# A two-layer decoder trunk in float32: the compression products packed into both column halves of the array

## The reference, cut to what matters

```
kv = (hn @ kv_w).reshape(B, S, 6, 4, 64)            # k_c = kv[:, :, 0], v_c = kv[:, :, 1]
n_cmp = (256 - 32) // 16 + 1                        # 15 blocks of 32 positions, 16 apart
idx = np.arange(n_cmp)[:, None] * 16 + np.arange(32)[None, :]
blocks = a[:, idx] + pos[None, None, :, None, :]    # a is k_c or v_c
blocks = blocks.transpose(0, 3, 1, 2, 4).reshape(B, 4, n_cmp, 32 * 64)
return jax.nn.silu(blocks @ w1) @ w2                # w1: 2048 x 256, w2: 256 x 64
```

## Time and profile before

| | |
|---|---|
| median of three executions | 1446.66 us |
| the profiled execution | 1446.41 us |
| its span (first to last record) | 1444.6 us |
| mean granted TensorE clock | 0.994 |
| PE, PEld, DVE, ACT, POOL busy | 96%, 54%, 30%, 20%, 5% of the span |
| chain that ended last | PE 73%, DMA 11%, SP's queue 10%, DVE 4% |

### The profile page before, as it was taken

How to read it: one execution, slowest core, us unless ns; L and a number is a source line. 1 busy time by engine, 2 the same in 40 slices (tenths; PEclk the granted TensorE clock), 3 DMA queues, 4 the chain that set the end, 5 groups by cost and what they waited for, 6 DMA issues and landing times.

```text
span 1444.6 us, 30800 instructions
## 1 busy us (share of the span) xinstructions
PE 1383.6 (96%) x13835; PEld 780.8 (54%) x13835; DVE 436.7 (30%) x668; ACT 292.7 (20%) x544; POOL 73.8 (5%) x124
## 2 busy tenths in 40 slices
PE   7999899999999898999979999999999999999986
PEld 6888778888777655334233254354354354336423
DVE  1489755554676834110100110110110210101020
ACT  4644444443643521000000000000000000000000
POOL 2000100000012001001001001001001001000100
PEclk9999999999999998999999999999999999999999
DMA  9423495547521806999999999999999999998997
GB/s 359 161 97 117 133 295 175 182 159 185 154 85 44 357 1 243 405 417 388 406 420 400 421 418 401 420 419 399 421 419 391 420 419 406 421 368 305 378 420 287
DMA packets 113123, 444.83 MB, mean 308 GB/s; under 512 B 11117, under 2 KB 37782, under 8 KB 82266
## 3 DMA queue, kind: packets, MB, share of 16 engines
q1 hardware_dynamic: 106160, 431.92, 76.8%
q0 software_dynamic: 3872, 10.49, 2.0%
q10 hardware_dynamic: 2954, 0.40, 0.2%
HBM read 433.85 MB, written 8.92 MB: 306 GB/s over the span
## 4 chain that ended last, share of the span: by engine, by line
PE 73%; DMA 11%; SPq 10%; DVE 4%; issue 1%; POOL 0%; ACT 0%; DVEq 0%; POOLq 0%; ACTq 0%
PE bank L2408 30%; PE bank L2415 10%; DMA ring<-in_moe_w_gu 9%; PE bank L2016 8%; SPq L622 5%; PE bank L2033 4%; SPq L618 4%; PE bank L1886 4%; PE bank L1927 3%; PE bank L2102 2%; DMA ring<-in_moe_w_down 2%; PE bank L2278 2%; PE bank L1908 2%; PE bank L1960 1%; PE bank L2172 1%
## 5 line engine op out<-in xcount | busy, mean ns | idle before, releaser
L2408 PE MATMUL bank<-ring,xT 128*32 128x384 f32 (+1 forms) x5888 | 559.5, 540 | 10.6 <-DMA ring<-in_moe_w_gu 10.4
L2408 PEld LDWEIGHTS bank<-ring,xT 128*32 128x32 f32 x5888 | 186.1, 110 | 378.6 <-issue 325.6
L2415 PE MATMUL bank<-ring,arena 128*32 128x256 f32 x5152 | 284.9, 380 | 16.9 <-DMA ring<-in_moe_w_down 16.9
L1788 DVE TENSOR_TENSOR arena<-arena,bank 128x384 f32<-128x384 f32 (+1 forms) x46 | 27.3, 593 | 734.6 <-PE bank L2408 734.6
L2415 PEld LDWEIGHTS bank<-ring,arena 128*32 128x32 f32 x5152 | 162.9, 110 | 141.2 <-DMA ring<-in_moe_w_down 31.5
L1303 DVE TENSOR_TENSOR ring_lo<-ring,f_whi 128x1024 fp32r<-128x1024 f32 x66 | 80.6, 1225 | 74.4 <-ACT f_whi L915 74.4
L1128 ACT ACTIVATE arena<-bank 128x384 f32<-128x384 f32 (+1 forms) x46 | 25.0, 544 | 380.6 <-PE bank L2408 380.6
L1134 ACT ACTIVATE arena<-bank 128x256 f32<-128x256 f32 x22 | 8.5, 385 | 452.6 <-PE bank L2415 452.0
L915 ACT ACTIVATE f_whi<-ring 128x1024 fp32r<-128x1024 f32 x66 | 69.8, 1062 | 78.4 <-PE bank L2016 48.1
L1886 PE MATMUL bank<-xT,ring 128*128 128x256 f32 x256 | 55.7, 380 | 0.0
L725 POOL DMA_DIRECT2D y_rows<-arena x28 | 15.1, 545 | 750.8 <-ACT arena L1134 750.8
(11 more groups left out here) (312 smaller groups left out, 1183.1 us busy)
## 6 DMA issues: line engine op xcount, KB each, us to landing
ring<-in_moe_w_gu SPq DMA_DIRECT2D x128, 1024.0 KB, 23.9
ring<-in_moe_w_down SPq DMA_DIRECT2D x112, 1024.0 KB, 27.1
ring<-in_moe_w_gu SPq DMA_DIRECT2D x128, 768.0 KB, 24.3
ring<-in_ffn_w_gu SPq DMA_DIRECT2D x22, 1024.0 KB, 7.8
ring<-in_hgrn_w_in SPq DMA_DIRECT2D x16, 1024.0 KB, 15.3
ring<-in_ffn_w_down SPq DMA_DIRECT2D x10, 1024.0 KB, 6.1
ring<-in_kv_w SPq DMA_DIRECT2D x6, 1024.0 KB, 6.3
ring<-in_hgrn_w_out SPq DMA_DIRECT2D x4, 1024.0 KB, 6.2
```

The source lines that it names most:

```text
L2408: last = mm(bank[32 * j:32 * j + 32, b, 0:WIDE[c]], m_xt[:, x, g, k, :], w[:, WIDE[c] * j:WIDE[c] * j + WIDE[c]], start=k == 0, stop=k == ...
L2415: last = mm(bank[32 * j:32 * j + 32, y, 0:256], m_t[c][:, g, b, :], w[:, b % 2, 256 * j:256 * j + 256], start=c == 0 and b == 0, stop=c == ...
```

## The change

There are five edits.

1. The products of odd j are written to partitions 64 to 123 of the same PSUM banks, that is, they use columns 64 to 123 of the array; even j stay in columns 0 to 59. Each half adds up 16 positions.
2. ACT copies both halves (60 x 256 each, for keys and values four copies where there were two silus) into `b_hs`, without the silu.
3. The four transposes (L2154) become four float32 products with all 128 partitions of `b_hs`: the moving operand is a constant of 60 columns, `C_FOLD`, with a one in row p and column p mod 64. It turns the tile and adds the halves. The constant makes the table `cf`, loaded at the start, 60 columns wider (from 631 to 691 floats in a row).
4. Partitions 60 to 63 and 124 to 127 of `b_hs` would enter that product, so DVE clears `b_hs` (128 x 512 floats) behind the additions of L1483, and ACT waits for it (`init_ok` 3).
5. The silu is done by ACT behind the product that turns (two of them, 128 x 120), straight into `b_hid`. DVE's two copies (L1501) are gone, and PE waits for `hid_ready` 2 from ACT.

```
@@ constants
-C_ALL = C_ONE + 1
+C_FOLD = C_ONE + 1
+C_ALL = C_FOLD + NG * NCMP
+    f[:, C_FOLD:C_FOLD + NG * NCMP] = p[:, None] % DH == np.arange(NG * NCMP)[None, :]
@@ ACT
             for kv in range(2):
                 act.wait_ge(hid_ps, kv + 1)
-                act.activation(b_hs[0:NG * NCMP, kv, :], bank[0:NG * NCMP, 4 + kv, 0:CH], ACT.Silu).then_inc(hs_ready, 1)
+                act.wait_ge(init_ok, 3)
+                for o in (0, DH):
+                    last = act.activation(b_hs[o:o + NG * NCMP, kv, :], bank[o:o + NG * NCMP, 4 + kv, 0:CH], ACT.Copy)
+                last.then_inc(hs_ready, 1)
+            act.wait_ge(hsT_ps, 2)
+            for kv in range(2):
+                act.activation(b_hid[:, kv, :, :].rearrange("p n (g c) -> p n g c", g=NG)[:, :, :, 0:NCMP],
+                               bank[:, 3, 256 * kv:256 * kv + 256].rearrange("p (n x) -> p n x", n=2)[:, :, 0:NG * NCMP]
+                               .rearrange("p n (g c) -> p n g c", g=NG), ACT.Silu).then_inc(hid_ready, 1)
@@ DVE
             last.then_inc(cin_ready, 1)
+            dve.wait_ge(cin_ready, 1)
+            dve.memset(b_hs, 0.0).then_inc(init_ok, 1)
             weight_low(12, 13)
...
             dve.wait_ge(init_ok, 2)
-            dve.wait_ge(hsT_ps, 2)
-            for kv in range(2):
-                last = dve.tensor_copy(
...
-            last.then_inc(hid_ready, 1)
@@ PE
-                    last = mm(bank[0:NG * NCMP, 4 + kv, 0:CH], b_cin[ps, j, :, :].rearrange("p g c -> p (g c)"),
-                              w[ps, j % 16, :], start=j == 0, stop=j == CB - 1)
+                    o = DH * (j % 2)
+                    last = mm(bank[o:o + NG * NCMP, 4 + kv, 0:CH], b_cin[ps, j, :, :].rearrange("p g c -> p (g c)"),
+                              w[ps, j % 16, :], start=j < 2, stop=j >= CB - 2)
...
-                    last = tp(bank[:, 3, P * n:P * n + NG * NCMP], b_hs[0:NG * NCMP, kv, P * half:P * half + P],
-                              ident[0:NG * NCMP, 0:NG * NCMP])
+                    last = mm(bank[:, 3, P * n:P * n + NG * NCMP], b_hs[:, kv, P * half:P * half + P],
+                              cf[:, C_FOLD:C_FOLD + NG * NCMP], start=True, stop=True)
...
-            pe.wait_ge(hid_ready, 1)
+            pe.wait_ge(hid_ready, 2)
```

More of the change, by code:

```diff
@@ L1498, in _ @@
             dve.wait_ge(init_ok, 2)
-            dve.wait_ge(hsT_ps, 2)
-            for kv in range(2):
-                last = dve.tensor_copy(
-                    b_hid[:, kv, :, :].rearrange("p n (g c) -> p n g c", g=NG)[:, :, :, 0:NCMP],
-                    bank[:, 3, 256 * kv:256 * kv + 256].rearrange("p (n x) -> p n x", n=2)[:, :, 0:NG * NCMP]
-                    .rearrange("p n (g c) -> p n g c", g=NG))
-            last.then_inc(hid_ready, 1)
             query_sums(0)
```

## The result

The changed kernel takes 1450.83 us in the median of 15 executions (1447.29 to 1452.53), the kernel before in the same sessions 1446.81 (1445.19 to 1449.75). The ratio of the times is 1.0019, 95% interval 1.001 to 1.0027: it is slower, by about 2.7 us by the ratio (the two medians lie 4.0 us apart; I go by the ratio, which comes with an interval). The forecast was 1444.2, faster. The profiled execution took 1451.04 us, its span is 1449.2.

The account below looks back on a forecast made before the run. Experts are bound by their weight stream, their start by PE's chain before it: query(0) 2.64 us earlier, plus 0.1 at the start, gives -2.5 us, so 1443.9 profiled and 1444.2 median; range over the cases 1442.8 to 1447.5.

Parts of the forecast that it names:

- What bounds the kernel: Experts' stage: bound by streaming weights; its start hangs on PE's chain, so each microsecond query(0) starts earlier is passed on.
- The compression products: Compression products on PE: 128 records in four array quarters take 7.0 us instead of 13.96, ending at 416.9.
- Rival A: Compression products: the four tiles don't run together, products stay at 14.0 us; 1447.3 us, chance 0.10.
- rival D: Compression products: four tiles together are slower than two, 18 us; 1451.5 us, chance 0.03.
- The wait for key 3: PE before key_turn(3): stands 3.8 us for DVE's last copy of key 3, which the clearing delays by 0.55 us.
- The product that turns: Between gates and query(0): eight float32 records replacing four transposes take 0.90 us instead of 0.39.
- The copies, the silu and the table load: On ACT: hidden, with cover of 2.4 us for the copies and over 4 us for the silu.
- The start: Load of the constant table, 9.5% wider: costs 0 to 0.6 us, taken as 0.1.
- From there: PE from key_turn(3) to query(0): gates keep 3.60 us, turning product 0.90; query(0) starts at 426.15, 2.64 us earlier.
- rival B: PE's wait near 421 us halves the clock: 1445.7 if short, 1451.2 if long; chance 0.16.
- the long fall: Clock low for 14 us after PE's wait: 4.5 us slower than before, 1451.2 us; chance 0.04.
- the short case: Clock low for about 3 us after PE's wait: gain shrinks to 1.0 us, 1445.7 us; chance 0.12.

Follow-up runs that it names:

- e1_fill: Changed kernel with seven unused float32 products filling PE's standstill before key_turn(3); 1445.07 us, ratio 0.9985 to the kernel before.
- e9_order: Kernel before, unpacked and without clearing, in the PE, DVE and ACT order of e8_mixed; 1447.12 us, ratio 0.9996 to the kernel before.
- e3_unpacked: Changed kernel with all positions' products in columns 0 to 59 again, the rest of the change kept; 1447.61 us, ratio 1.0006 to the kernel before.
- e4_gates: Changed kernel with the gate products moved ahead of key_turn(3), into the standstill; 1445.74 us, ratio 0.9987 to the kernel before.
- e5_chain: e4_gates with DVE's clearing moved behind key 3's last copy and key 2's copy moved earlier; 1442.39 us, ratio 0.9965 to the kernel before.
- e2_half: Kernel before with the compression products of odd positions left out, 64 records instead of 128; 1448.43 us, ratio 1.001 to the kernel before.
- e8_mixed: Changed kernel reordered, halves of query(0) alternating with gates and key_turn(3) on PE, DVE and ACT reordered too; 1441.85 us, ratio 0.9957 to the kernel before.

## Why the prediction was wrong

*What bounds the kernel*: right. The experts are bound by their weights, and what delays or hastens PE at the end of `query(0)` arrives at their start within 0.7 us in the profiles of all six versions that have `query(0)` in one piece (in the changed kernel 3.8 us at the one, 3.4 at the other). The differences of the profiles and of the ratios in the table also go together within 0.7 us, but for e1_fill and e9_order.

*The compression products*: right. 7.07 us for 128 records, 0.055 a record, against the 7.0 forecast from the strips. Rival A and rival D are gone. By the Trainium skill, "TensorE: Matmul & The Clock Gate", in its part on packing tiles, loads overlap running products only when the row group differs. Two of the four tiles here share each row group, the 128 loads lie within 6.68 us beside the products, and the rate still doubled, so the measurement decides against that rule for this shape.

*The wait for key 3*: right, in place, cause and size: 3.60 us, forecast 3.8, ended by the copy forecast; the clearing costs 0.61, forecast 0.55.

*The product that turns*: right, 0.88 (e3_unpacked), forecast 0.90. *The copies, the silu and the table load*: hidden as said; ACT's four copies, 1.55 us, first matter in e4_gates and e5_chain, where PE waits 0.5 us for them. *The start*: the table's piece of the chain is 6.08 us after and 6.36 before, so a cost of 0.1 is not to be seen.

*From there*: wrong, and this is the step that failed. It counted on a granted clock of 1.00 behind the wait, and let the gates keep 3.60 us, the product that turns 0.90 and `query(0)` its 5.66. They took 6.71, 1.69 and 7.85, together 6.1 us more, for the clock was at half during all of the first two and 5.0 us of the third: 3.1 in the gates, 0.8 in the product that turns, 2.2 in `query(0)`. The forecast of -2.6 us and these 6.1 make +3.5; measured at the end of `query(0)` it is 28.4 against 24.6, +3.8. This is rival B, the fall of 13.7 us, of which the prediction gave place, length (14 us) and price (4.5 us, 1451.2). The price was too high: 3.4 us in the profile and 2.7 by the ratio. That the profiled execution has 1451.04 is in part chance, for of its 4.6 us above before 0.8 lie ahead of the change and 0.4 behind the start of the experts. The prediction gave the long fall a chance of 0.04. The reason against it was that unbroken work stands behind the gap. It does, but for its first 8.4 us, to `query(0)`, it is gates with 48 moving columns and the product that turns, and the clock was low during all of it. The row ahead of the fall at 553.5 has 3.52 of 4 us busy, with products of 8 moving columns and four transposes; the text named both these columns and the gaps, and its argument for the short case used only the gaps.

What the experiments leave of the theory: taking work away ahead of this stretch is enough to bring the fall (e2_half), filling the standstill turns the sign (e1_fill, e4_gates), and in these runs the gain came in full only where the stretch without long products is also short (e5_chain) or broken up by the queries (e8_mixed). In e1_fill and e4_gates the clock fell during or behind the gates with little or no standstill before it, so the standstill alone is not the cause. Nor is the length of the stretch without long products alone: it was 4.9 us in before (423.90 to 428.79) and 6.3 in e5_chain with the clock at 1.00, while in e1_fill the clock fell 3.3 us after such a stretch began (420.2 to 423.5). The products that filled the gap of e1_fill had the identity as weights and constants as moving data, half of them the identity again, so mostly zeros; whether products of real data would have kept the clock up was not tried. What exactly the clock gate asks for is open; no run here was made to find it. Open too is why e8_mixed gained 5.3 us over e9_order and not the 6.5 by which its attention starts earlier (`query(1)` ends 24.4 against 30.9 us after the first product, in the profiles); with 7 and 12 executions scattered over 3 to 4 us the difference may be no more than that scatter.

## What to carry to other kernels

Before TensorE's work is shortened, look at what stands next on it: what it then waits for, and whether the work behind that is long products or narrow ones. A busy share of 100% is no sign that the clock will stay up (e1_fill was busy for the whole of the microsecond in which it fell). Where the shortened work leaves a stretch of transposes, narrow products and waits, move long products into it in the same step, and read the mean granted clock of every execution beside the time; here the same edit was worth +2.7 us or, with the order changed, about -6, of which the order alone gave nothing that can be told (e9_order).

## What the runs showed of the hardware

- Float32 products on quarters of the array (64 rows by 60 columns, 256 moving columns) run four at a time: 0.055 us a record (128 in 7.07 us), against 0.109 for row halves (128 in 13.96 us), with loads and products of two tiles in the same row group side by side (128 loads in 6.68 us).
- A kernel with less work was slower: half of the compression products left out (e2_half), +1.4 us by the ratio.
- The clock fell with PE busy. In e1_fill it had stood 0.58 us in the 14 us ahead of the fall, and had been doing products with 48 moving columns for 2.3 us when it fell; it came back 6.8 us later, 3 us into the queries. In the changed kernel, after 3.60 us of standstill, it was low for 13.7 us, 5 us of them into the queries.
- The mean clock of an execution was nearly the same in all executions of a kernel with a long fall (0.988 to 0.990 in all 15 of the changed kernel and all 11 of e2_half), but not in e1_fill (0.990 to 0.995), whose times scatter over 6.6 us. Where the clock was low is known of the profiled executions only.
